# Second block's token mixer on one Trainium2 core: values computed token-major, pool means on GpSimd, input blocks taken head by head

## The reference

```python
h = rmsnorm(x, mix_norm[l])
p = h @ w_in[l]                    # 2048 columns: a 256, f 256, q 512, k 512, v 512
y_pool = pool_mixer(a, pool_w[l], pool_scale[l])
y_four = fourier_mixer(f, fourier_w[l])
y_attn = diff_attention(q, k, v, lam, lam_init, attn_head_norm[l])
y = jnp.concatenate([y_pool, y_four, y_attn], axis=-1) @ w_out[l]
x = x + y
```

## Time and profile before

| | |
|---|---|
| median of 3 runs | 1996.58 us (1996.06 to 1996.93) |
| the profiled execution | 1996.7 us, its span 1994.9 us |
| PE busy | 1977.5 us, 99% |
| DVE, ACT, POOL busy | 1428.5, 1019.3, 150.8 us |
| granted TensorE clock, mean | 0.999 |
| chain of work that ended last | PE 88%, DVE 5%, ACT 3% |

### The profile page before, as it was taken

The page is one execution under the profiler, slowest core; times in us unless marked ns, Lnnn a source line. Parts: engine busy times, 40 slices in busy tenths (PEclk is TensorE's granted clock), DMA queues, the critical chain, the costliest instruction groups (busy, mean ns, idle before and its releaser), DMA issues.

```text
span 1994.9 us, 42299 instructions
## 1 busy us (share of the span) xinstructions
PE 1977.5 (99%) x16154; PEld 1938.0 (97%) x16154; DVE 1428.5 (72%) x2593; ACT 1019.3 (51%) x1525; POOL 150.8 (8%) x190
## 2 busy tenths in 40 slices
PE   9999999999999999999999999999999999999998
PEld 9999989999999999899999999999999999999998
DVE  6674887886688768878868775667756775667763
ACT  4433686544455447765446444564444443555443
POOL 0001122000100011210010000010000000100000
PEclk9999999999999999999999999999999999999999
DMA  7454423545454544245554664335464555435554
GB/s 258 171 203 167 169 85 128 190 168 195 156 179 176 188 150 166 84 171 190 191 188 143 222 229 170 137 136 195 179 220 165 190 197 194 147 124 183 189 208 150
DMA packets 46830, 346.66 MB, mean 174 GB/s; under 512 B 5344, under 2 KB 6416, under 8 KB 9232
## 3 DMA queue, kind: packets, MB, share of 16 engines
q1 hardware_dynamic: 44416, 335.63, 46.8%
q0 software_dynamic: 2320, 9.74, 1.5%
HBM read 344.29 MB, written 1.07 MB: 173 GB/s over the span
## 4 chain that ended last, share of the span: by engine, by line
PE 88%; DVE 5%; ACT 3%; DVEq 1%; issue 1%; ACTq 0%; DMA 0%; SPq 0%; POOL 0%
PE ps L580 28%; PE ps L582 28%; PE ps L581 28%; DVE w_lo L1894 2%; ACT w_hi L1223 1%; ACT scratch L1571 1%; ACT cst L1561 1%; DVE cst L2362 0%; PE ps L1123 0%; PE ps L1088 0%; DMA raw<-in_w_up 0%; PE ps L812 0%; DVE pj L2341 0%; DVE scratch L2308 0%; DVE plain L2005 0%
## 5 line engine op out<-in xcount | busy, mean ns | idle before, releaser
L1894 DVE TENSOR_TENSOR w_lo<-raw,w_hi 128x1024 fp32r<-128x1024 f32 (+1 forms) x582 | 748.5, 1312 | 170.7 <-ACT w_hi L1223 168.7
L1223 ACT ACTIVATE w_hi<-raw 128x1024 fp32r<-128x1024 f32 (+1 forms) x582 | 634.9, 1121 | 140.5 <-PE ps L582 126.3
L580 PE MATMUL ps<-x_hi,w_lo 128*128 128x256 f32 (+2 forms) x2416 | 693.4, 287 | 2.7 <-DVE x_lo L1981 1.4
L582 PE MATMUL ps<-x_hi,w_hi 128*128 128x256 f32 (+2 forms) x2416 | 685.8, 284 | 0.0
L581 PE MATMUL ps<-x_lo,w_hi 128*128 128x256 f32 (+2 forms) x2416 | 681.2, 282 | 0.0
L580 PEld LDWEIGHTS ps<-x_hi,w_lo 128*128 128x128 f32 x2416 | 454.7, 188 | 11.2 <-issue 6.6
L581 PEld LDWEIGHTS ps<-x_lo,w_hi 128*128 128x128 f32 x2416 | 455.4, 188 | 0.8
L582 PEld LDWEIGHTS ps<-x_hi,w_hi 128*128 128x128 f32 x2416 | 454.5, 188 | 0.0
L580 PE MATMUL ps<-hid_hi,w_lo 128*128 128x256 f32 (+1 forms) x1536 | 435.5, 284 | 0.7 <-DVE hid_lo L2092 0.4
L581 PE MATMUL ps<-hid_lo,w_hi 128*128 128x256 f32 (+1 forms) x1536 | 434.0, 283 | 0.0
L582 PE MATMUL ps<-hid_hi,w_hi 128*128 128x256 f32 (+1 forms) x1536 | 433.4, 282 | 0.0
(11 more groups left out here) (331 smaller groups left out, 1537.4 us busy)
## 6 DMA issues: line engine op xcount, KB each, us to landing
raw<-in_w_up SPq DMA_DIRECT2D x176, 1024.0 KB, 4.8
raw<-in_w_down SPq DMA_DIRECT2D x64, 1408.0 KB, 6.1
raw<-in_w_in SPq DMA_DIRECT2D x36, 1024.0 KB, 4.8
raw<-in_w_out SPq DMA_DIRECT2D x16, 1024.0 KB, 4.8
cst<-row_copy POOLq DMA_DIRECT2D x2, 1088.0 KB, 8.7
raw<-in_w_up SPq DMA_DIRECT2D x4, 512.0 KB, 6.9
cst<-in_consts POOLq DMA_DIRECT2D x1, 1537.5 KB, 6.3
prm<-in_prm POOLq DMA_DIRECT2D x2, 690.0 KB, 7.5
```

Of the source, the lines that this page charges most:

```text
L580: mm(dst, w_lo[:, j, cols], xa, start=first, stop=False)
L582: return mm(dst, w_hi[:, j, cols], xa, start=False, stop=last)
L1223: fn(w_hi[:, j, c], raw[:, j, c], ACT.Copy).then_inc(hi_done, 1)
L1894: v.tensor_tensor(w_lo[:, j, c], raw[:, j, c], w_hi[:, j, c].bitcast(F32), ALU.subtract)\
```

## The change

**Order of the blocks.** `w_in`'s blocks (and the weights packed on the host) stand in a new order: q and k of head 0, the two pool blocks, q and k of head 1, the two Fourier blocks, q and k of heads 2 and 3, then the values. The islands follow: `att_s(0)` comes after block 3, each `att_t` about one head later.

**Values.** The four value blocks are no longer computed feature-major, scaled by DVE and transposed. `value_tokens(pair, i)` takes 128 tokens of `xt_hi` or `xt_lo` as the stationary operand and two value blocks of the weights, 2 x 128 columns, as the moving one, again 24 matmuls of 256 columns. The result is token-major; ACT copies it to `vtok` with `rstd` as a scale per partition, which `rstd_columns` (two matmuls of one column, one ACT copy) turns over once. `unit_used` rises by two at the end of the second call of a pair.

**Pool means.** The transposes, the copies and the band product on PE are gone. `window_means` on POOL builds window sums of 2, 4, 8 and 16 from shifted adds, multiplies by 1/count and subtracts `a`. It stands ahead of `fold_tokens` on that engine. `pool_out` stands in the middle of the mixer.

**Buffers.** `attn_t` has a part for each head, so `at_copy` waits for no `att_o`; some PSUM banks are moved. `pool_out` no longer waits for `o2_rstd`, and `mean_squares` waits for all four value copies (`v_ready`).

```diff
-F0, A0 = 0, 14
-Q, K, V = (2, 4, 6, 8), (3, 5, 7, 9), (10, 11, 12, 13)
-CAT_ORDER = (2, 3, 4, 5, 6, 7, 0, 1)
+F0, A0, V0 = 6, 2, 12
+Q, K, V = (0, 4, 8, 10), (1, 5, 9, 11), (12, 13, 14, 15)
+CAT_ORDER = (2, 3, 0, 1, 4, 5, 6, 7)
...
+                def value_tokens(pair, i):
+                    n = V0 + 2 * pair
+                    turn, j, bank = turn0 + n // 4, (n // 2) % 2, (n + i) % IN_BANKS
...
+                    pe.wait_ge(lo_done, turn * 4 + (2 * j + 2))
+                    both_hi, both_lo = (w[:, j, 0:2 * W_NARROW].rearrange("p (u w) -> p u w", u=2) for w in (w_hi, w_lo))
+                    dst, t = ps[:, bank, 0:256], slice(P * i, P * i + P)
+                    for k in range(KD):
+                        c = slice(k * P, k * P + P)
+                        mm(dst, xt_hi[:, k, t], both_lo[:, :, c], start=k == 0, stop=False)
+                        mm(dst, xt_lo[:, k, t], both_hi[:, :, c], start=False, stop=False)
+                        last = mm(dst, xt_hi[:, k, t], both_hi[:, :, c], start=False, stop=k == KD - 1)
+                    if i == 0:
+                        last.then_inc(v_done.sem, 1)
+                    else:
+                        last.then_inc(unit_used, 2)
...
                 def mean_squares(pair):
 
-                    pe.wait_ge(proj2_ready.sem, proj2_ready.at(l, (14, 16)[pair]))
+                    pe.wait_ge(v_ready.sem, v_ready.at(l, 4))
```

PE's list of calls, which stands in place of the one printed above:

```diff
+                rstd_columns()
+                att_s(0)
                 block(4)
+                block(5)
+                block(6)
+                att_s(1)
+                att_t(0)
+                block(7)
+                block(8)
                 feature_sums()
...
+                value_tokens(0, 0)
                 fourier_out()
+                pool_out()
                 att_s(3)
+                value_tokens(0, 1)
+                att_t(2)
+                value_tokens(1, 0)
                 att_o(0)
                 att_o(1)
+                att_t(3)
+                value_tokens(1, 1)
                 mean_squares(0)
...
-                return {1: a_transposes, 2: last_output, 3: last_means, 4: pool_out}
+                pe.wait_ge(nm2_ready.sem, nm2_ready.at(l, 4 * ATT_HEADS))
+
+                return {1: lambda: att_o(2), 2: lambda: att_o(3), 4: lambda: mean_squares(1)}
```

POOL's new function, called ahead of `fold_tokens(l)`:

```diff
+            def window_means(l):
+                two, four = windows
+                a = pj[:, A0:A0 + 2, :]
...
+                pool.wait_ge(proj2_ready.sem, proj2_ready.at(l, A0 + 2))
+                nc.gpsimd.tensor_tensor(two[:, :, 1:T1], a[:, :, 0:T1 - 1], a[:, :, 1:T1], ALU.add)
+                pool.drain()
+                nc.gpsimd.tensor_tensor(four[:, :, 2:T1 - 1], two[:, :, 1:T1 - 2], two[:, :, 3:T1], ALU.add)
+                pool.drain()
+                eight, sixteen = two[:, 1, :], four[64:P, 1, :]
...
+                    nc.gpsimd.tensor_tensor(poolm[rows, :, :], sums[rows, :, inner], count, ALU.mult)
+                pool.drain()
+                nc.gpsimd.tensor_tensor(poolm, poolm, a[:, :, inner], ALU.subtract).then_inc(pm_ready.sem, 1)
```

More of the change, by code:

```diff
@@ L105 @@
 CC_W = _n
-CC_FIRST = CC["band"]
+CC_FIRST = CC["rcount"]
 AL_W = ATT_HEADS * 2 * 256
@@ L149, in shape_constants @@
     put("one", np.ones((P, 1)))
-    band = np.zeros((4, 256, 256))
+    rcount = np.zeros((P, 2, T2))
     for g, w in enumerate(POOL_WINDOWS):
[L152 to L156, removed]
+        t = np.arange(T2)
+        count = np.minimum(t + w - w // 2, T2) - np.maximum(t - w // 2, 0)
+        rcount[64 * (g % 2):64 * (g % 2) + 64, g // 2, :] = 1.0 / count
+    put("rcount", rcount.reshape(P, -1))
     t, s = np.arange(1, P + 1), np.arange(HALF)
@@ L452, in build @@
         attn = take(2, 2, T2)
-        atok = take(2, T2)
         used[0] = NF * T1 + KD * T2
         vtok = take(2, 512)
-        attn_t = take(2, 2, T2)
         sqo = take(4, T2)
         poolm = take(2, T2)
+        windows = [cst[:, CC["rest"] + 2 * T1 * i:CC["rest"] + 2 * T1 * (i + 1)].rearrange("p (a t) -> p a t", a=2)
+                   for i in range(2)]
+        attn_t = cst[:, CC["rest"] + 4 * T1:CC["rest"] + 4 * T1 + 8 * T2].rearrange("p (h k t) -> p h k t", h=ATT_HEADS, k=2)
+        assert CC["rest"] + 4 * T1 + 8 * T2 <= CC_W
         y_squares = scr[:, 14 * T2:22 * T2].rearrange("p (k t) -> p k t", k=KD)
@@ L1050, in fourier_out @@
                     last.then_inc(f3_done.sem, 1)
[L1052 to L1071, removed]
@@ L1079, in pool_out, with rstd_columns @@
                                   poolm[head_rows(g), g // 2, :], start=True, stop=True)
                     last.then_inc(py_done.sem, 1)
+                def rstd_columns():
+                    pe.wait_ge(std_ready, norm + (3 * DEPTH + 1))
+                    for i in range(2):
+                        last = mm(ps[:, 6, 508 + i:509 + i], rstd[0:1, P * i:P * i + P], con("one", 1, slice(0, 1)),
+                                  start=True, stop=True)
+                    last.then_inc(rstd_t.sem, 1)
@@ L2627, in mixer2 @@
                 weights(6)
+                maxima(0)
                 scale(4)
@@ L2661, in mixer2 @@
                 norm_o(1)
-                scale(15)
-                weights(18)
-                weights(19)
                 att_low(0)
                 att_low(1)
+                weights(18)
                 norm_o(2)
```

193 lines of the change are left out of this document (86 added, 107 removed).

## The result

The changed kernel takes **1998.66 us**, median of 22 runs (1997.71 to 2000.48), the kernel before on the same chip 1995.93, median of 22 (1995.12 to 1997.83). The ratio is 1.0013, 95% interval 1.0007 to 1.0019: slower by 2.7 us, 0.13%, where 2001.3 was forecast. Its profiled execution took 1998.41 us for a span of 1996.3.

The account below looks back on a forecast made before the run. PE, busy for 99% of the span, was taken to bound the kernel. Per mixer, work -3.2, old waits -0.95 and new waits 1.4, 1.3, 0.9, 0.3, 0.6, 2.0 gave +2.35 us, hence 2001.3 us, range 1996.0 to 2006.5.

Parts of the forecast that it names:

- The forecast case: Likeliest case: PE waits at the mixer's end and DVE held up by POOL, 1999.8 to 2005.2 us, chance 0.60.
- Work off PE: Band product, transposes and changes of kind leave PE, two one-column matmuls come in: -3.2 us per mixer.
- Old waits: PE's earlier waits, ahead of `att_s(2)` and in and behind the first output pair, vanish: -0.95 us per mixer.
- The first pair: Output projection: PE waits for head 2's low part, with only 12 matmuls to fill the chain: +1.4 us per mixer.
- The third block: Output projection: the residual add stands behind the split of unit 19 on DVE, so PE waits: +1.3 us per mixer.
- `mean_squares(0)`: First mean squares wait for the copy of the last value product: +0.9 us per mixer.
- `att_t(3)`: Head 3's transposes wait, DVE and ACT work of 8.1 us against PE's 7.8: +0.3 us, bounds 0 and 0.8.
- `feature_sums`: Behind the Fourier blocks, POOL's fold has only block 8 to hide in: +0.6 us per mixer, bounds 0 and 1.5.
- `att_t(0)`: Head 0's transposes wait for DVE's difference, held up by POOL's window sums: +2.0 us per mixer, bounds 0 and 4.3.
- The first rival: POOL waits for DVE, never DVE for POOL where it counts: +0.35 us per mixer, 1997.3, chance 0.24.
- Rival two: The mixer's end is covered and both end waits vanish: -2.35 us per mixer, 1991.9, chance of faster 0.08.
- The two dear ones: POOL slower than its rows, 2016 us, chance 0.04; value products slower than blocks, up to +7 us per mixer, chance 0.04.

Follow-up runs that it names:

- Experiments 4: Changed kernel with the split of unit 19 right behind that of unit 18 on ACT and DVE: 1997.28 us against 1995.84, ratio 1.0007.
- experiment 6: Changed kernel, tail rearranged: first mean squares wait for three copies, `att_o` and last mean squares earlier, squares ahead of high parts: 1993.64 us against 1996.36, ratio 0.9988.
- experiment 3: Changed kernel with the first mean squares waiting for three copies of values instead of four: 1997.04 us against 1995.84, ratio 1.0006.
- experiment 1: Changed kernel without POOL's window sums, only a last subtraction giving zeros: 1995.55 us against 1995.84, ratio 0.9999.
- experiment 5: Changed kernel with the window sums behind the fold and waiting for head 1's difference: 1995.94 us against 1996.36, ratio 1.0001.
- experiment 2: Changed kernel with the window sums behind the fold on POOL instead of ahead of it: 1999.73 us against 1995.84, ratio 1.0020.
- Experiment 8: Changed kernel with 256 neighbouring columns as the value products' moving operand instead of two pieces of 128: 1998.9 us in a single run.
- experiment 9: Changed kernel with the mixer's ordinary blocks given a moving operand of two pieces of 128 columns: 2000.26 us in a single run.
- experiment 10: Changed kernel with each matmul triple reordered so no two neighbours share the stationary operand, whole kernel: 1998.88 us against 1996.27, ratio 1.0013.

## Why the prediction was right in its direction, and 2.6 us too high

The recorded range holds the result and the direction is right, but the size is not the likeliest one. The forecast case alone reached from 1999.8 to 2005.2 us, +1.6 to +4.3 per mixer, and 1998.66 with +1.26 lies below it; "slower by over 0.2%" had 0.58, and what came, 0.13%, lies in the part that had 0.34. The time is nearer to the 1997.3 of the case in which POOL costs nothing than to 2001.3; the waits, and not the time, show that POOL does cost.

For one mixer the forecast was work -3.2, old waits -0.95, new waits +6.5, together +2.35. Measured: +1.26. By its steps:

- **Work off PE: -3.2, measured about -3.05.** The band product, the transposes of `a` and those of values went as priced, 2.9. `rstd_columns` stands 0.53 us wide (1258.36 to 1258.89) where 0.3 was taken, and the eight matmuls of `fourier_out` take 1.82 instead of 1.54. Against that the other small products became 0.5 us shorter together, several now standing side by side, and the blocks and value products together shrank by some 0.45 us beyond the waits in them, most of it the closer value products. I had counted the changes of kind with 0.6 and the values with nothing: that they "can't be cheaper than the block rate" was wrong, they stand 0.1134 us apart.
- **Old waits: -0.95, as measured**: 0.4 ahead of `att_s(2)` and about 0.55 in the first pair and behind it. -3.05 - 0.95 and the new waits below, +5.25, make the +1.26.
- **The first pair: +1.4, measured 1.6.** The listed wait is 1.34, but the restart is 3.10 us behind the first of 12 matmuls that take 1.5 with the change of kind. **The third block: +1.3, measured 1.25** (the restart is 2.66 us behind the first of 12 matmuls that take 1.41; the listed wait is 0.98). Both were read off the chain of links, each at its measured length, and came out within 0.2. Experiments 4 and 6 show that these are two waits with two causes: a split out of place, and a chain with too little cover.
- **`mean_squares(0)`: +0.9, measured 0.7.** Right place and cause (experiment 3); the listed wait is 0.56 and the row stands 0.72 late.
- **`att_t(3)`: +0.3, measured 0.** The transposes start at 1304.52, right behind the 1.90 us of `att_o`. The two estimates 8.1 and 7.8 were closer than their errors.
- **`feature_sums`: +0.6, measured about 0.2.** Block 7's successor starts at 1274.53 and the sums at 1277.62, 3.09 us later where a block takes 2.83. POOL's fold took the 1.64 and 0.73 that were forecast; what failed was the 0.4 between a block's last matmul and its scale, which starts at 1274.72, 0.2 behind.
- **`att_t(0)`: +2.0, measured 1.5.** The mechanism was right: experiment 1 takes it away, experiment 5 keeps POOL's work and takes it away. The make-up of the number was not. The sum had three meetings, 0.6, 0.6 and 1.0, less 0.2 to spare, and counted splits and the two-operand difference. DVE lost 1.04 at the split and 0.76 at the `tensor_scalar` on two elements, which the sum had left out, less some 0.3 to spare; the meeting with the two-operand difference never came, since POOL was done at 1269.66, before 1270.26, and not near 1271. So part of the nearness of 2.0 to 1.5 is luck. POOL was early for several small reasons: it began at 1258.97 and not 1259.3, and it lost 0.91, 0.94 and 0.93 to splits where 1.05 and two or three times 1.1 were counted. Its own time was nearly right by two errors that cancel. I drew POOL's cost per element as a line through 256 and 272 elements, two points too close to give a slope, and got 1.3 us for 512 to 542, where 538 take 1.08 (1261.11) and the pair of 512 some 1.25 each; and I left no gap between the operations, where each stands 0.14 us behind the one before. That makes 7.9 us against 8.1.

Of the new waits, `att_t(0)`, `feature_sums`, `att_t(3)` and `mean_squares(0)` were put 1.4 us too high together, and the first pair 0.2 too low. Two of these four, `att_t(0)` and `att_t(3)`, are waits that could not be read off a row, and for which I took a value well above nothing. The first rival (POOL waits, but never DVE at a place that counts) gave +0.35 per mixer; experiments 1 and 5, where that is so, stand at -0.2 (66.5 against 66.77). Rival two, that the end is covered, needed the chain half as long; experiment 6 got there by giving it more cover instead. The two dear ones are out by the rows: POOL's long sums take 1.1 to 1.3 us each alone, and the value products run faster than blocks.

The forecast gave the Trainium skill's rule (SBUF — State Buffer, "Who interferes with whom") by which a `tensor_scalar` can be locked out as well, and had no row for it. This case now shows it: 0.99 us for 0.23, and in experiment 2 0.98 for the pair at 0.61. The same section says that a DVE instruction with at most one SBUF input outside the 2-port modes does not contend; the scale at 1282.67 (0.41 beside POOL) agrees. Its 2.6 us for this wait was too high all the same, since it stood on the 2.0 with the meeting that never came. Without the loss at the `tensor_scalar`, by an estimate from these rows, the two-operand difference would have started some 0.76 us earlier, lost 0.15 to POOL's end at 1269.66, and left a wait of 0.9.

## What to carry to other kernels

Work moved from a full PE to an idle engine is worth its length on PE (here 3.0 us a mixer) only if nobody on PE waits for what that engine holds up: find who stands behind the held instruction, and gate the idle engine's work behind the last one that matters (experiment 5, one wait, 1.5 us a mixer). A short piece of PE work between a reduction and its consumer is cover, so before taking it out lay the chain's links end to end at their measured lengths and see what is left to fill them; and let a wait name the producer that is needed, not the last of its group (experiment 3, 0.7 us for one constant).

## What was not expected of the hardware

- **The value products stand 0.1134 us apart, blocks 0.1177**, both with 256 moving columns at a mean granted clock of 0.999. In the first 24 of them the three matmuls of a chunk take 0.34 us. What differs is that activations are stationary and weights move. Experiment 8 and experiment 9 rule out the pieces of the moving operand, experiment 10 the repeated stationary operand. What in the exchange of operands does it stays open. The later groups, behind a change of kind, take 2.85 and 2.86 us for 24 where a block behind one takes 2.91 to 3.00.
- **POOL's `tensor_tensor` does not cost twice as much for twice the elements**: 0.74 us for 256, 1.08 for 538, 1.09 for 542 (experiments 2 and 5). With 0.14 us between one and the next, many small ones are dearer than the elements say.
- **Two elements are held up as a thousand are**: a DVE `tensor_scalar` of 0.23 us lost 0.76 to POOL.
